# The recurrent half of an output projection: plain fp32 operands in place of three products of rounded parts

## What is computed

```
h = modulate(rmsnorm(x))                        # latents and context
f, xr, gr = split(h @ w_in)                     # 512 columns each
fourier_out = fourier_mix(f)                    # (512 tokens, 512)
rg_out = rglru(xr) * gelu(gr)                   # (512 tokens, 512), the recurrent group
cat = concat([rmsnorm(fourier_out, g_out_f), rmsnorm(rg_out, g_out_r)], axis=-1)
x = x + gt_m * (cat @ w_out)                    # w_out: 1024 x 1024
h = modulate(rmsnorm(x, g_norm_ffn))
x = x + gt_f * moe_ffn(h)                       # router, top 4 of 32 experts, clamped SwiGLU
out = rmsnorm(x, g_final)
```

## Time and profile before

| | before |
|---|---|
| median of 3 runs | 1492.31 us |
| lowest, highest | 1492.02, 1496.39 us |
| the profiled execution | 1493.59 us |
| its span, first to last instruction | 1491.7 us |
| mean granted clock of TensorE in it | 0.959 |
| busy share PE, DVE, ACT, POOL | 89%, 61%, 43%, 17% |
| Fourier half, TensorE | 208.7 to 232.2 us |
| recurrent half, TensorE | 235.7 to 259.2 us |
| routing done, first expert item | about 308 us |

### The profile page before, as it was taken

How to read it: one execution, slowest core, us unless ns; L and a number is a source line. 1 busy time by engine, 2 the same in 40 slices (tenths; PEclk the granted TensorE clock), 3 DMA queues, 4 the chain that set the end, 5 groups by cost and what they waited for, 6 DMA issues and landing times.

```text
span 1491.7 us, 25997 instructions
## 1 busy us (share of the span) xinstructions
PE 1326.8 (89%) x6235; PEld 536.1 (36%) x6235; DVE 905.7 (61%) x1451; ACT 648.5 (43%) x724; POOL 254.4 (17%) x156
## 2 busy tenths in 40 slices
PE   4699879589999999999879987799999999999991
PEld 2587458533333333333223322233332333333330
DVE  2899886755556565555445543555555556565555
ACT  3333742234544444454334433345444544445443
POOL 1741253211111111111110100111111111111111
PEclk9799979589999999999999999999999999999996
DMA  9665222789999999699999999999997299999993
GB/s 379 227 212 207 101 111 80 280 279 372 380 380 380 378 390 376 198 375 382 382 385 377 385 380 381 386 384 364 382 381 258 62 380 382 377 384 377 393 383 136
DMA packets 207765, 477.51 MB, mean 320 GB/s; under 512 B 18562, under 2 KB 19074, under 8 KB 206722
## 3 DMA queue, kind: packets, MB, share of 16 engines
q1 hardware_dynamic: 196914, 458.39, 82.9%
q0 software_dynamic: 10832, 18.90, 5.6%
HBM read 464.11 MB, written 20.45 MB: 325 GB/s over the span
## 4 chain that ended last, share of the span: by engine, by line
PE 45%; SPq 26%; DVE 8%; DMA 8%; issue 8%; ACT 3%; POOL 1%; DVEq 1%; ACTq 0%; POOLq 0%
PE ps L1498 23%; SPq L320 20%; PE ps L1510 9%; DMA ring<-in_w_down 6%; SPq L323 4%; DVE window L1037 2%; DMA wm<-in_w_mod 2%; PE ps L1314 2%; PE ps L1315 2%; PE ps L1316 2%; PE ps L1490 1%; PE ps L1480 1%; PE ps L1402 1%; PE ps L1403 1%; PE ps L1404 1%
## 5 line engine op out<-in xcount | busy, mean ns | idle before, releaser
L1498 PE MATMUL ps<-window,xT 128*64 128x512 f32 x2880 | 645.9, 597 | 27.1 <-DVE window L1037 19.1
L1037 DVE COPY window<-ring 128x2048 f32 (+1 forms) x364 | 444.3, 1227 | 315.7 <-PE ps L1510 104.3
L1510 PE MATMUL ps<-window,aT 128*64 128x512 f32 x1440 | 340.8, 602 | 30.9 <-DVE window L1037 18.5
L759 ACT ACTIVATE window<-ring 128x2048 f32 x180 | 340.0, 1908 | 50.6 <-DMA ring<-in_w_down 38.0
L1498 PEld LDWEIGHTS ps<-window,xT 128*64 128x64 f32 x2880 | 196.4, 137 | 406.3 <-issue 349.5
L753 ACT ACTIVATE sg<-gb 128x256 f32<-128x256 f32 x90 | 37.5, 416 | 424.2 <-DVE gb L1184 424.2
L563 POOL DMA_INDIRECT y_rows<-osb,idx_c x46 | 78.0, 1695 | 633.9 <-ACT osb L749 619.4
L1510 PEld LDWEIGHTS ps<-window,aT 128*64 128x64 f32 x1440 | 90.6, 136 | 187.5 <-issue 133.4
L1184 DVE TENSOR_SCALAR gb<-ps 128x256 f32<-128x256 f32 x90 | 38.2, 424 | 170.7 <-PE ps L1498 170.7
L550 POOL DMA_INDIRECT xg<-h_rows,idx_n x46 | 65.3, 1420 | 412.2 <-DVE idx_n L1074 386.6
L749 ACT ACTIVATE osb<-ps,gate_c 128x512 f32<-128x512 f32 x46 | 31.7, 688 | 119.9 <-PE ps L1510 119.2
(11 more groups left out here) (292 smaller groups left out, 1166.8 us busy)
## 6 DMA issues: line engine op xcount, KB each, us to landing
ring<-in_w_gate_up SPq DMA_DIRECT2D x512, 512.0 KB
ring<-in_w_down SPq DMA_DIRECT2D x128, 1024.0 KB
wm<-in_w_mod SPq DMA_DIRECT2D x4, 2048.0 KB, 21.8
wm_a<-in_w_mod SPq DMA_DIRECT2D x4, 2048.0 KB, 9.1
wm_b<-in_w_mod SPq DMA_DIRECT2D x4, 2048.0 KB, 8.7
win<-in_w_in SPq DMA_DIRECT2D x3, 2048.0 KB, 20.1
x_in<-in_x SPq DMA_DIRECT2D x1, 2048.0 KB, 10.7
wo_f<-in_w_out SPq DMA_DIRECT2D x1, 2048.0 KB, 7.8
```

The costliest lines, as they stand in the source:

```text
L759: A(window[c % NW][:, :, :, :], ring_chunk(c, p), ACT.Copy).then_inc(S["moved_by_act"], 1)
L1037: V.tensor_copy(window[c % NW][:, :, :, :], ring_chunk(c, p)).then_inc(S["moved_by_dve"], 1)
L1498: last = MMUL(ps[M * j:M * (j + 1), h, :].rearrange("m (g n) -> m g n", g=2), xT[:, k, :], window[c % NW][:, k % CK, :, j * GW:(j + 1) * G ...
L1510: last = MMUL(ps[M * y:M * (y + 1), 2, :], aT[:, h, i, M * j:M * (j + 1)], window[c % NW][:, k % CK, y, :], start=False, stop=(h == 1 and ...
```

## The change

The recurrent half multiplies the scaled heads and the loaded weights as plain fp32, one matmul in place of three. Gone are the rounding of the recurrent weights on VectorE, their low part on GpSimd, and the low part of the heads on VectorE. ScalarE writes the scaled heads as fp32 and not rounded (same place, same size). TensorE waits for the heads of each `k` before its first use, and for the weights' load. The Fourier half computes what it did; its function has the parts written out. Products, banks and the order of tiles are otherwise the same.

```diff
-        wo_hi = [at("wo_f_hi", [P, 2, GT, CH], SLOT[3], F32R), at("wo_r_hi", [P, 2, RT, CH], SLOT[0], F32R)]
-        wo_lo = [at("wo_f_lo", [P, GT, D], ZD, F32R), at("wo_r_lo", [P, RT, D], ZD + 16 * KB, F32R)]
-        catR = [at("catR_hi", [P, RT, NL], ZA + 16 * KB, F32R), at("catR_lo", [P, 2, RT, NB], SLOT[1] + 8 * KB, F32R)]
+        wo_f_hi = at("wo_f_hi", [P, 2, GT, CH], SLOT[3], F32R)
+        wo_f_lo = at("wo_f_lo", [P, GT, D], ZD, F32R)
+        catR = at("catR", [P, RT, NL], ZA + 16 * KB)
...
 # GpSimd
             pool.dma_start(rows(y_dram), zero[:, 0:YW].unsqueeze(1).to_broadcast([P, TL * CG, YW])).then_inc(S["scattered"], 16)
-            wo_part(1, 0)
-            wo_part(1, 1)
...
 # ScalarE
-                A(catR[0][:, t, :], Um[:, 0, t, NC:], ACT.Copy, scale=pc[:, COLS["g_r"][0] + t:COLS["g_r"][0] + t + 1]).then_inc(S["catR_hi_ready"], 1)
+                A(catR[:, t, :], Um[:, 0, t, NC:], ACT.Copy, scale=pc[:, COLS["g_r"][0] + t:COLS["g_r"][0] + t + 1]).then_inc(S["catR_ready"], 1)
...
 # VectorE
-            round_wo(1)
             rstd_heads(0, "ssf_done")
 
-            for t in range(RT):
-                dve.wait_ge(S["catR_hi_ready"], t + 1)
-                V.scalar_tensor_tensor(catR[1][:, 0, t, NC:], Um[:, 0, t, NC:], pc[:, COLS["g_r"][0] + t:COLS["g_r"][0] + t + 1],
-                                       catR[0][:, t, :].bitcast(F32), ALU.mult, ALU.subtract).then_inc(S["catR_lo_ready"], 1)
...
 # TensorE
+            def out_bank(t, n):
+                return ps[:, 2 * (1 + t % 3) + n, :]
+
+            def project_fourier(t):
+                for n in range(2):
+                    if t == 0:
+                        pe.wait_ge(S["wo_lo_ready"], n + 1)
+                    for k in range(GT):
+                        hi, lo = [c[:, k, t * P:(t + 1) * P] for c in catF]
+                        w_h, w_l = wo_f_hi[:, n, k, :], wo_f_lo[:, k, n * CH:(n + 1) * CH]
+                        MMUL(out_bank(t, n), hi, w_h, start=(k == 0), stop=False)
+                        MMUL(out_bank(t, n), hi, w_l, start=False, stop=False)
+                        last = MMUL(out_bank(t, n), lo, w_h, start=False, stop=(k == GT - 1))
+                last.then_inc(S["pf_done"], 1)
+
+            def project_recurrent(t):
+                for n in range(2):
+                    for k in range(RT):
+                        if t == 0 and n == 0:
+                            pe.wait_ge(S["catR_ready"], k + 1)
+                        last = MMUL(out_bank(t, n), catR[:, k, t * P:(t + 1) * P], wo[1][:, k, n * CH:(n + 1) * CH],
+                                    start=(k == 0), stop=(k == RT - 1))
+                last.then_inc(S["pr_done"], 1)
...
-            pe.wait_ge(S["catR_lo_ready"], RT)
+            pe.wait_ge(S["ld_wo1"], 16)
             pe.wait_ge(S["ld_wr"], 32)
             for t in range(TL):
                 pe.wait_ge(S["pf_copied"], (TL, 2, 3)[t] if t < 3 else TL)
                 if t >= 3:
                     pe.wait_ge(S["pr_read"], t - 2)
-                project_out(1, t, lambda k, t: [catR[0][:, k, t * P:(t + 1) * P], catR[1][:, 0, k, NC + t * P:NC + (t + 1) * P]], "pr_done")
+                project_recurrent(t)
```

More of the change, by code:

```diff
@@ L301, in build @@
             dft_done cf_copied ssf_done sp_ready ix_ready a_ready th_ready q_ready w_ready root_ready
-            rg_ready sqr_ready ssr_done mean_heads root_heads rsf_ready cf_lo catR_hi_ready catR_lo_ready
+            rg_ready sqr_ready ssr_done mean_heads root_heads rsf_ready cf_lo catR_ready
             wo_hi_ready wo_lo_ready pf_done pf_copied pr_done pr_read x2_ready ssq_ffn rt_ffn h_scaled
@@ L513, in _, with wo_part @@
                 nc.gpsimd.tensor_tensor(Qm[n % 2][:, :], Am[:, d, t, :], Am[:, d, t, :], ALU.mult).then_inc(S["q_ready"], 1)
[L515 to L521, removed]
+            def wo_part(n):
+                pool.wait_ge(S["wo_hi_ready"], n + 1)
+                nc.gpsimd.tensor_tensor(wo_f_lo[:, :, n * CH:(n + 1) * CH], wo[0][:, :, n * CH:(n + 1) * CH],
+                                        wo_f_hi[:, n, :, :].bitcast(F32), ALU.subtract).then_inc(S["wo_lo_ready"], 1)
+            wo_part(0)
+            wo_part(1)
             pool.wait_ge(S["ix_ready"], 3 * RT)
@@ L973, in _, with round_wo @@
             drive(1)
-            def round_wo(i):
-                dve.wait_ge(S[f"ld_wo{i}"], 16)
+            def round_wo():
+                dve.wait_ge(S["ld_wo0"], 16)
                 for n in range(2):
-                    V.tensor_copy(wo_hi[i][:, n, :, :], wo[i][:, :, n * CH:(n + 1) * CH]).then_inc(S["wo_hi_ready"], 1)
+                    V.tensor_copy(wo_f_hi[:, n, :, :], wo[0][:, :, n * CH:(n + 1) * CH]).then_inc(S["wo_hi_ready"], 1)
             dve.wait_ge(S["ix_ready"], 4 * RT)
-            round_wo(0)
+            round_wo()
             for g in range(GT):
@@ L1391, in square_sums @@
                 last.then_inc(S[name], 1)
-            def project_out(i, t, heads, name):
+            def out_bank(t, n):
+                return ps[:, 2 * (1 + t % 3) + n, :]
+            def project_fourier(t):
                 for n in range(2):
                     if t == 0:
-                        pe.wait_ge(S["wo_lo_ready"], 2 * i + n + 1)
+                        pe.wait_ge(S["wo_lo_ready"], n + 1)
                     for k in range(GT):
[L1399 to L1405, removed]
+                        hi, lo = [c[:, k, t * P:(t + 1) * P] for c in catF]
[12 more added lines that the diff above has]
+                last.then_inc(S["pr_done"], 1)
             pe.wait_ge(S["cf_copied"], GT)
@@ L1413, in _ @@
                     pe.wait_ge(S["pf_copied"], t - 2)
-                project_out(0, t, lambda k, t: [c[:, k, t * P:(t + 1) * P] for c in catF], "pf_done")
+                project_fourier(t)
             pe.wait_ge(S["sqr_ready"], RT)
             square_sums(1, lambda g, t: Um[:, 1, g, NC + t * P:NC + (t + 1) * P], "ssr_done")
-            pe.wait_ge(S["catR_lo_ready"], RT)
+            pe.wait_ge(S["ld_wo1"], 16)
             pe.wait_ge(S["ld_wr"], 32)
```

## The result

The changed kernel takes 1496.46 us (median of 11 runs, 1493.62 to 1500.61) against 1492.28 us for the kernel before (11 runs, 1490.52 to 1496.39): ratio 1.0026, 95% interval 1.0017 to 1.0036, so 2.5 to 5.4 us slower. The forecast was 1495.1 us, 2.8 us slower. The profiled execution of the changed kernel took 1495.75 us, its span is 1493.9.

The account below looks back on a forecast made before the run. The expert loop fills most of the span (DMA 98% busy) and is untouched; only its start moves. Tile 1's delay of 2.83 us passes on, other terms add 0: from 1492.31 to 1495.1 us, range 1491.0 to 1499.0.

Parts of the forecast that it names:

- The price of a plain call: TensorE, recurrent half: a plain fp32 call is two records, 0.858 us against 0.681 for three products; a tile 1.41 us longer.
- The two ends: Bounds on a plain call's cost: at most 1.9 us from the low-clock gates, 0.46 us from the expert products.
- The clock: TensorE, tile 0 of the recurrent half: a low stretch of the same length, its 1.7 us loss dropping out of the difference.
- The rival of a longer stretch: Clock stays low longer in tiles 0 and 1: 1496.8 us if twice as long, 1507 if throughout; chance 0.07.
- Removed work worth 0: Rounding and low parts taken off VectorE and GpSimd lay beside TensorE's full stretch before the recurrent half; gain 0.
- Only tile 1's delay goes on: VectorE behind the recurrent half: of TensorE's 5.65 us only tile 1's 2.83 us pass on; tile 3 is covered by 4 us.
- The rows of tile 0 on VectorE: VectorE's first steps with GpSimd's 2.40 us cast meeting the second; tile 0 done at about 249.5 us, before tile 1 arrives.
- The same work after it at the same clock: TensorE after the recurrent half, 262 to 310 us: same work, clock 0.52 as before, so the 2.83 us pass through unchanged.
- The load queue: First four expert chunks issued twice the shift later, 265.1 to 269.3 us; at worst 2.8 us late, hidden by a 5.47 us wait.
- The sum: Expert loop's start and the end move by 2.8 us: 1495.1 us, 0.19% more; no-change band 1487.8 to 1496.8, chance of same 0.75.
- signs of being wrong: Logits shifting under 1.7 or over 4 us, a tile not 6.86 us at full clock, or end and loop start shifting differently.
- the stalls rival: VectorE's stalls behind GpSimd line up otherwise: 1.7 us left if one falls away, nearly nothing with two; 1492.6 to 1494.0; chance 0.12.

Follow-up runs that it names:

- rot_plain: The changed kernel with the recurrent square sums issued inside token tile 0 and the output banks turned by one; ratio to the kernel before 1.0014.
- kept_work: The changed kernel with the removed VectorE and GpSimd rounding and low-part work put back, written where nobody reads; ratio to the kernel before 1.0019.
- pad_tile3: The kernel before with 24 more idle fp32r products, 5.45 us, all in token tile 3 of the recurrent half; ratio 1.0001.
- pad_each: The kernel before with six more idle fp32r products in every token tile of the recurrent half, 5.45 us in all; ratio 1.0022.
- defer_before: The kernel before with GpSimd's low part of the bias rows put off until VectorE has made the last normed tile; ratio 0.9975.
- rot_defer_three: The kernel before (three products) with square sums inside tile 0, GpSimd's low part of the bias rows put off and banks turned by one; ratio 0.9972.
- sums_in_plain: The changed kernel with the recurrent square sums issued inside token tile 0, two calls ahead of each plain product; ratio to the kernel before 1.0023.
- sums_defer: The changed kernel with square sums inside tile 0 and GpSimd's low part of the bias rows put off; ratio to the kernel before 0.9998.

## Why the prediction was right

*The price of a plain call, 0.858 us.* Right: 0.430 us a record in the changed kernel against 0.429 from the inverse transform. The two ends kept beside it had no part in it. A call as long as four of today's products, 0.908 us, is out too: tile 2 follows tile 1 after 6.87 us, and it would have been 7.26. A call left two records as long as this; what the array does within them the trace doesn't show.

*The clock.* Right: one low stretch of the same depth and place, its loss out of the difference. The rival of a longer stretch did not come. The runs with the sums inside tile 0 put a number on it: without the block of one-column products the clock stays up and rot_plain gains 1.69 us.

*Removed work worth 0.* Right, shown by kept_work. The prediction set the ends of the work, 231.1 and 232.95, against the end of the square sums at 235.73, and the low parts of the heads need that cover: they end 0.7 us after E. It didn't say that the square sums are the cover, nor that they also stand over the copy of Fourier tile 3. The change left them where they were, so it cost nothing here.

*Only tile 1's delay goes on.* Right, and it is the step that mattered: 2.91 us at tile 1 and 2.87 at the logits against 2.83, while TensorE's half grew by 5.8. pad_tile3 shows it from the other side.

*The rows of tile 0 on VectorE.* Off without effect. The cast was put at 2.40 us and its meeting with the second step at over a microsecond. The cast takes 1.47 us when it starts beside VectorE's step from PSUM; the 2.40 of rows 8 are those of a cast that started during VectorE's second step, and hold a wait for it (below). So tile 0 was done at 248.3 and not 249.5, and the idle time ahead of tile 1 was 2.70 us and not 1.8.

*The same work after it at the same clock.* Not quite. TensorE pauses only 2.1 us between the first two turned tiles, where it paused 5.0 us before, and the second turn (1.09 us) and the first router products (1.96) run at the full level; the clock from 262 to 310 us is 0.59 and was 0.52. In the kernel before the second turn was:

```profile
265.28 1.97 PE L1432 MATMUL ps<-csb,h_sb 128*128 128x128 f32 x8 [5.03 <-POOL h_sb L539]
```

The router products after those wait 5.99 us for ScalarE's copy, which follows VectorE's tile 3, so nothing came of it.

*The load queue.* Right: chunks 5.8 us later, no wait at their copies.

*The sum.* 2.83 us was forecast for the median, 4.2 us lie between the medians, and the interval of 2.5 to 5.4 holds both the forecast and the 2.87 of the trace. kept_work and pad_each, with the same delay, came out at 1.0019 and 1.0022. I take 2.9 us for the change; the rest up to 4.2 shows in no stage and is within what the runs scatter. The prediction gave "same" 0.75, with a band up to 1496.8. The median, 1496.46, lies 0.3 us below that edge, 1.4 us above the forecast: the delay was right, but that the runs stayed within the band took some luck. None of the signs of being wrong came: the logits shift by 2.87 us (1.7 to 4 allowed), a tile takes 6.87 us, and the end of the execution shifts by 2.6 us after E where the start of the loop shifts by 2.7. One bound of the stalls rival was added up wrongly: 2.83 - 2.2 = 0.6 us gives 1492.9, not 1492.6; nothing hangs on it.

## What to carry to other kernels

A longer product costs only what it adds ahead of the last place where another engine waits for TensorE and doesn't win the wait back behind it (the 0.27 us before tile 2 were won back in the step after): find that place in the consumer's idle time, tile by tile, and price the delay there, 2.9 us of 5.8 here. Count records, not calls, before comparing precisions: one plain fp32 call was two records of 0.43 us, dearer than three fp32r products of 0.227. And before moving work that looks like overhead ahead of a stage, list what it covers: 3.5 us of one-column products stood over a wait of 1.6 us for a bank's copy, and only with the banks turned did the move pay, 1.7 us in the trace.

## What the runs showed of the hardware

*One-column products cost as much between long ones as in a block.* Four one-column records between plain calls cost 0.44 us, 0.11 each, the same as 32 of them in a block (3.48 us). The expectation had added up the loads of all records and compared the sum with the long products' time. (It counts 32 plain records where tile 0 has 16; 16 x 0.19 + 32 x 0.11 = 6.6 us is still below tile 0's 6.86, so by its rule nothing should have been added.) An explanation that fits, but was not tried by itself: a long product covers the one load that follows it, and the loads behind short products stand free, however the records are mixed. The Trainium skill's page "TensorE: Matmul & The Clock Gate" (LDWEIGHTS) gives a load P / 1.2 ns for P columns, 107 ns for 128; the 0.109 us of a one-column record agree.

*The block of one-column products alone is followed by the low clock.* In all six kernels that have the block (the one before, the changed one, kept_work, both padded ones and defer_before) the clock is 1.00 while it runs and falls once the long products have begun: 0.59 and 0.57 in the 4 us above, 0.57 and 0.61 from 234 to 238 us in kept_work and pad_tile3. In the six with the same records spread among long products it stays at 1.00 through the half.

*A VectorE step with both inputs in SBUF that starts while a GpSimd instruction runs waits until this has ended.* In five places of the kernel before and again in the changed one its end is 1.1 us after GpSimd's, whenever the step began: 259.17 + 2.00 against 257.73 + 2.35 in the changed kernel, 256.36 + 2.39 against 255.28 + 2.39 before. The copies of the chunks, with one input, wait as well: in defer_before the four take 7.86 us in place of 4.62. GpSimd waits for VectorE in the same way (the cast takes 1.47 us in one trace and 2.40 in the other, where it starts at 244.76, during a step that ends at 245.84). The steps that read PSUM don't wait: the one at 257.85 in the changed kernel starts while GpSimd's addition runs and takes its 1.28 us.

*The start of the half differs by 4 us between the traces.* E lies at 229.67 in rot_plain and 233.62 in rot_defer_three, with the same work ahead on TensorE. The stretch from 60 to 100 us tells the difference:

```profile
60.00:100.00 40.00, 37.74 (x212) 32.86 (x211) 38.87 (x40) 9.26 (x14) 17.54 (x13) 1.00 0.61 215
```

```profile
60.00:100.00 40.00, 36.77 (x196) 32.49 (x196) 38.87 (x39) 7.61 (x13) 19.97 (x13) 0.91 0.61 214
```

The clock is 1.00 in the one and 0.91 in the other, and (1.00 - 0.91) x 40 = 3.6 us, most of the 3.95 between them: a low stretch falls among the input projection's products, or does not. The other traces fit: with 1.00 there (kept_work, pad_tile3, sums_in_plain) E is 229.6 to 230.1, with 0.96 (the other seven) 231.8 to 232.4. This is only a part of the scatter. The span from the logits to the end differs too, 1202.6 to 1206.1 us over the twelve traces, with 1206.1 in sums_defer, whose profiled execution of 1496.73 us lies 4.8 above its median. Each trace is of another kernel, so that runs of one kernel (1490.52 to 1496.39 us for the one before) differ for the same reasons is likely, not shown. A difference of 3 us needs distances within the trace or many runs.
